# Extra products of constants on TensorE inside its waits, in a two-model transformer kernel on one Trainium2 core

## The chip, the cores and the metric

The kernel runs on one core of a Trainium2 chip. Its time is the device time of one launch in microseconds (us). Three runs of the kernel before gave 2714.12 us as their median, from 2710.6 to 2715.03 us.

## What is computed

A sequence of 256 tokens of width 1024 passes through two models, all in float32. The first has two layers; each is a SwiGLU feed-forward network (1024 to 2816 and back), a mixer, a cross attention to 256 memory tokens, and a second feed-forward network, with an RMS norm ahead of each part. The mixer of layer 0 has windowed attention with sinks beside stick-breaking attention; that of layer 1 is a dilated attention with 16 heads. The second model has two layers whose norms are scaled and shifted by vectors made from a conditioning input. Its mixer is a hybrid of three attentions, and after it comes a dense feed-forward network in layer 0 and a mixture of 8 experts, two per token, in layer 1. Cut to what matters:

```python
for layer in range(2):                       # first model
    x = x + 0.5 * swiglu_ffn(rms_norm(x), ...)
    x = x + mixer[layer](rms_norm(x), ...)
    x = x + memory_cross_attention(rms_norm(x), mem, ...)
    x = x + 0.5 * swiglu_ffn(rms_norm(x), ...)
for layer in range(2):                       # second model
    h = rms_norm(x) * (1 + sc1) + sh1
    x = x + gt1 * hybrid_mixer(h, ...)
    h = rms_norm(x) * (1 + sc2) + sh2
    x = x + gt2 * (swiglu(h, ...) if layer == 0 else moe_swiglu(h, ...))
return rms_norm(x)
```

## The kernel before, in words

A plan (`make_plan`) lists the stages in order, and every engine has its own program that walks through that list; semaphores tie the programs together. Tokens are held in two row tiles (b = 0, 1) of 128 each, and the width in 8 blocks (k) of 128. Weights stream through a ring of seven 1 MB slots (ten in the experts) that SyncE fills; a slot is refilled when TensorE has used what was in it. PSUM has eight banks of 128x512 float32, and each stage has a fixed use of them. One matmul of float32 stands in the trace as two instructions of the same shape; counts such as x16 are of those.

TensorE's program, the only one that the change touches, is one strict order of instructions:

- **norm** (L1112). For each row tile it waits for x (`x_at`), then turns 8 blocks of x (L1108, 16 instructions) into banks 0 to 3. In an "early" norm it then waits for VectorE's diagonal matrix of the row scales (L2504), multiplies it by ones (L1119) into bank 7, and the next stage starts. VectorE copies that row (L2507) and writes xT block by block (L2513, and L2518 where there is a shift); the next stage's first products (L1231 of a feed-forward network, L1815 of the hybrid mixer) follow block by block on the count `xT_k`. The norms ahead of the feed-forward networks and of the hybrid mixers are early, seven in all. The others ("late") apply the row scale afterwards; the one ahead of the router is "raw".
- **feed-forward** (L1217): the first pair of tiles by plain products (L1231 gate, L1234 up), then a seven-product form (L1274), then the product with the second weight (L1325).
- **attn** (L1584), the attentions with sinks (4 bodies of two heads) and dilated (8 bodies). Staged copies of queries and keys, made by GpSimd, are turned (L1577) into banks 4 and 5; scores (L1603) go to banks 0 and 1; weights are turned (L1617) into banks 2 and 3; outputs (L1629) go to bank 6. Pieces of the memory's keys and values for the later cross attention (`kv_piece`, L1553, bank 7) stand between these steps: one piece (sinks) or two (dilated) before body 0, and the others beside the bodies.
- **stick** (L1650), stick-breaking attention, with the later-sums (L1682) into banks 2 and 3.
- **hybrid** (L1798): pieces of the input projection (L1815, banks 5 and 7), ten pairs of heads, and pieces of the output projection (L1836). At pair 5, `turn_diff` (L1907) waits for `diff_done`, VectorE's normalised output of the difference heads (L2676), turns it (L1912) into bank 5, and then come scores (L1893) of pair 6.
- **route and experts**: 16 products with 8 columns for the router (L2022), a wait for `chosen_ready` (VectorE's choice of experts), five products with 8 columns (L2002 to L2006), the gathering products of expert 0 (L1369), whose results ScalarE moves to SBUF (L2279), and then the experts' products (L1418, L1461), whose weights come at the rate of the DMA.

`cst` is a table of constants in SBUF, loaded at the kernel's start, and `ident` its first 128 columns. A wait of TensorE's program holds back all that stands behind it, as here in `outputs` of attn:

```python
                    for b in range(NB):
                        pe.wait_ge(sm[f"p_ready{b}"], w + 1)     # L1613: exponentials are there
                        pe.wait_ge(sm[f"pt_evac{b}"], w)         # L1614: bank 2 + b is free
```

Of the kernel before, what the change touches and what calls it, by code (L numbers as in the profile page):

```python
# [423 lines left out]
def build(nc, A, out, stop=None):  # L424
    plan, released, landed, places, before = make_plan(stop)
    ctx = ExitStack()
    with ctx:
# [668 lines left out]
        def _(pe):  # L1096
# [3 lines left out]
            def transposes_of(src, done, ready=None):  # L1100

                rows = src.rearrange("p b (q k) -> p b k q", k=KT)
                for b in range(NB):
                    if ready is not None:
                        ready(b)
                    for half in range(2):
                        for j in range(4):
                            ins = nc.tensor.transpose(banks[2 * b + half][:, j * P:(j + 1) * P],  # L1108
                                                      rows[:, b, half * 4 + j, :], ident)
                        ins.then_inc(done, 1)  # L1110

            def norm(st):  # L1112
                n0 = st["n0"]
                last = [max(i for i, (pb, _) in enumerate(pieces(st["order"])) if pb == b) for b in range(NB)]
                transposes_of(x[:, :, :], sm["norm_psum"], lambda b: x_at(pe, st, last[b]))
                if st["how"] == "early":
                    pe.wait_ge(sm["diag_ready"], st["early"] + 1)
                    for b in range(NB):
                        ins = mm(banks[7][:, b * P:(b + 1) * P], C("ones"), diag[:, b, :], start=True, stop=True)  # L1119
                    ins.then_inc(sm["rsb_psum"], 1)  # L1120

# [234 lines left out]
            def experts(st):  # L1356
# [42 lines left out]
                def gate_up(e, i, between):  # L1399
                    n, groups = 3 * e + i, GROUPS_OF[e]  # L1400
                    w = CHUNKS[i][1]
                    for k in range(KT):
# [3 lines left out]
                        if k == 0:  # L1406
                            pe.wait_ge(sm["gath_evac"], 2 * (e + 1))
# [176 lines left out]
            def attn(st):  # L1584
# [7 lines left out]
                def scores(i):  # L1592
# [3 lines left out]
                    staged_out(u)  # L1596
                    for b in range(NB):
                        pe.wait_ge(sm[f"s_read{b}"], w)

# [8 lines left out]
                def outputs(i):  # L1608
                    u, w = i + st["n0"]["pairs"], i + st["n0"]["soft"]
                    beside(i, 2, 6)  # L1610
                    for b in range(NB):
                        nt = b + 1
                        pe.wait_ge(sm[f"p_ready{b}"], w + 1)  # L1613
                        pe.wait_ge(sm[f"pt_evac{b}"], w)  # L1614
# [20 lines left out]
                for n in side["first"]:  # L1635
                    kv_piece(st, n, 0, KT)
                scores(0)
# [12 lines left out]
            def stick(st):  # L1650
# [24 lines left out]
                def later(i):  # L1675

                    w = i + n0["stick"]
                    for h in range(2):
                        pe.wait_ge(sm[f"sp_done{h}"], w + 1)
                        pe.wait_ge(sm[f"arg_done{h}"], w)  # L1680
# [117 lines left out]
            def hybrid(st):  # L1798
# [108 lines left out]
                def turn_diff():  # L1907
                    pe.wait_ge(sm["diff_done"], l + 1)
                    pe.wait_ge(sm["w2_evac0"], nb * (l + 1))
# [66 lines left out]
            for i_st, st in enumerate(plan):  # L1976
# [3 lines left out]
                if kind == "norm":  # L1980
                    norm(st)
# [17 lines left out]
                elif kind == "experts":  # L1999

                    pe.wait_ge(sm["chosen_ready"], 1)
# [1537 lines left out]
```

## Time and profile before

| what | us |
|---|---|
| median of three runs (lowest, highest) | 2714.12 (2710.6, 2715.03) |
| time of the profiled execution | 2716.32 |
| its span, first to last instruction | 2714.4 |
| TensorE busy | 2573.7 (95%) |
| VectorE busy | 1291.6 (48%) |
| ScalarE busy | 438.0 (16%) |
| GpSimd busy | 200.9 (7%) |
| mean granted TensorE clock | 0.983 of full speed |
| HBM traffic over the span | 227 GB/s |

1.9 us of the profiled execution's time lie outside its span. The page also has the busy share and TensorE's granted clock by fortieths of the span, and the chain of work that ended last. Other views used below: the timeline (start, duration, engine, line, operation, out<-in, shapes, count; in brackets the engine's idle time before it and what ended that), the waits of an engine, and windows, which give each engine's busy time, the granted clock, the DMA share and GB/s in a stretch.

### The profile page before, as it was taken

What the parts mean: (1) busy time and instruction counts of PE and PEld (TensorE: products, weight loads), DVE (VectorE), ACT (ScalarE), POOL (GpSimd) and SP (SyncE); (2) the same over time, 40 slices, a digit from 0 to 9 for tenths busy, and PEclk for the clock granted to TensorE, in tenths of its full rate; (3) what the DMA queues carried; (4) which work ended last, traced back from release to release, by engine and by line L of the source; (5) the groups of instructions that cost most, each with busy time, mean ns of one, the idle gap of its engine ahead of it and who ended that gap; (6) DMA issues with size and microseconds to landing.
All of it is one profiled execution on the core that took longest, in us unless ns stands there. A gap on an engine that the chain in (4) does not pass through costs nothing.

```text
span 2714.4 us, 44439 instructions
## 1 busy us (share of the span) xinstructions
PE 2573.7 (95%) x18246; PEld 1684.7 (62%) x18246; DVE 1291.6 (48%) x2756; ACT 438.0 (16%) x1199; POOL 200.9 (7%) x330
## 2 busy tenths in 40 slices
PE   8999899999999998999999989999989999989996
PEld 8964457797599444577964659945655335624452
DVE  5887342478877854325887536664531000000102
ACT  1201252010012013221101321102311001101010
POOL 3010100000000102000011110001100000000000
PEclk9999999999999999999999999999989999999999
DMA  8684323367556733234675324543359999999997
GB/s 286 212 312 161 109 94 124 114 218 251 208 194 229 245 139 124 79 108 149 218 258 149 123 101 164 181 161 114 116 186 382 413 412 413 416 413 411 411 414 314
DMA packets 306524, 619.19 MB, mean 228 GB/s; under 512 B 15948, under 2 KB 172784, under 8 KB 306192
## 3 DMA queue, kind: packets, MB, share of 16 engines
q1 hardware_dynamic: 287088, 550.80, 54.9%
q0 software_dynamic: 19232, 65.52, 7.4%
q8 instruction: 147, 2.41, 0.3%
q14 instruction: 57, 0.47, 0.1%
HBM read 607.47 MB, written 8.79 MB: 227 GB/s over the span
## 4 chain that ended last, share of the span: by engine, by line
PE 69%; issue 10%; DVE 9%; DMA 6%; SPq 3%; ACT 1%; POOL 1%; DVEq 0%; POOLq 0%; ACTq 0%
PE psum L1274 22%; PE psum L1418 10%; PE psum L1815 6%; PE psum L1461 5%; PE psum L1325 4%; PE psum L1553 3%; DMA xn<-in_w_ada 2%; PE psum L1190 2%; PE psum L1142 2%; PE psum L1726 2%; PE psum L1836 2%; DMA ring<-in_w_exp_up 2%; PE psum L1231 2%; DVE proj L2874 1%; DMA ring<-in_w_exp_down 1%
## 5 line engine op out<-in xcount | busy, mean ns | idle before, releaser
L1418 PE MATMUL psum<-ring,xT 128*32 128x512 f32 (+3 forms) x3372 | 293.3, 494 | 15.6 <-DMA ring<-in_w_exp_up 13.9
L3370 DVE SCALAR_TENSOR_TENSOR proj<-proj,psum 128x256 f32<-128x256 f32 (+1 forms) x63 | 24.8, 394 | 558.1 <-ACT proj L2294 558.1
L1418 PEld LDWEIGHTS psum<-ring,xT 128*32 128x32 f32 x3372 | 129.3, 110 | 166.5 <-issue 114.2
L1274 PE MATMUL psum<-xT,ring 128*128 128x128 f32 x1600 | 195.0, 275 | 0.0
L1274 PEld LDWEIGHTS psum<-xT,ring 128*128 128x128 f32 x1600 | 187.7, 192 | 4.1 <-issue 3.8
L1815 PE MATMUL psum<-ring,xT 128*128 128x384 f32 (+1 forms) x448 | 157.8, 502 | 2.9 <-DVE xT L2518 2.9
L2874 DVE SCALAR_TENSOR_TENSOR proj<-xn,cols,proj 128x512 f32<-128x512 f32 x168 | 126.0, 750 | 17.6 <-DMA xn<-in_w_ada 13.5
L1553 PE MATMUL psum<-ring,memT 128*128 128x512 f32 x256 | 121.4, 614 | 7.3 <-issue 7.3
L1815 PEld LDWEIGHTS psum<-ring,xT 128*128 128x128 f32 x448 | 82.3, 192 | 61.9 <-issue 13.6
L938 POOL DMA_DIRECT2D xn<-in_w_ada x96 | 69.4, 724 | 686.5 <-DVE proj L2874 679.9
L1461 PE MATMUL psum<-ring,proj 128*32 128x256 f32 x1872 | 104.6, 379 | 0.0
L1325 PE MATMUL psum<-ring,proj 128*128 128x512 f32 x220 | 102.6, 592 | 0.0
L1274 PE MATMUL psum<-qT,ring 128*128 128x128 f32 x800 | 98.0, 276 | 1.4 <-DVE picked L3068 1.4
L1274 PE MATMUL psum<-diff_o,ring 128*128 128x128 f32 x800 | 97.5, 275 | 0.0
L1274 PEld LDWEIGHTS psum<-qT,ring 128*128 128x128 f32 x800 | 93.3, 192 | 5.6 <-DVE picked L3068 5.6
L1461 PEld LDWEIGHTS psum<-ring,proj 128*32 128x32 f32 x1872 | 73.8, 110 | 31.5 <-issue 6.1
L1274 PEld LDWEIGHTS psum<-diff_o,ring 128*128 128x128 f32 x800 | 93.3, 192 | 0.0
L2187 ACT ACTIVATE silu<-pT 128x256 f32<-128x256 f32 x100 | 41.8, 418 | 292.8 <-DVE pT L2996 185.1
L1553 PEld LDWEIGHTS psum<-ring,memT 128*128 128x128 f32 x256 | 47.2, 196 | 58.7 <-issue 58.4
L2294 ACT ACTIVATE proj<-psum 128x256 f32<-128x256 f32 (+1 forms) x63 | 23.0, 366 | 345.3 <-PE psum L1418 345.3
L1325 PEld LDWEIGHTS psum<-ring,proj 128*128 128x128 f32 x220 | 41.4, 190 | 50.2 <-issue 50.2
L1836 PE MATMUL psum<-ring,memT 128*128 128x512 f32 x128 | 63.4, 630 | 0.9 <-ACT memT L2092 0.9
(534 smaller groups left out, 4287.6 us busy)
## 6 DMA issues: line engine op xcount, KB each, us to landing
ring<-in_ffn_w_gu SPq DMA_DIRECT2D x88, 1024.0 KB, 7.3
ring<-in_w_exp_down SPq DMA_DIRECT2D x62, 1024.0 KB, 16.8
xn<-in_w_ada POOLq DMA_DIRECT2D x96, 512.0 KB, 4.8
ring<-in_ffn_w_down SPq DMA_DIRECT2D x44, 1024.0 KB, 7.7
ring<-in_w_exp_gate SPq DMA_DIRECT2D x82, 512.0 KB, 11.5
ring<-in_w_exp_up SPq DMA_DIRECT2D x82, 512.0 KB, 15.5
ring<-in_w_exp_gate SPq DMA_DIRECT2D x52, 384.0 KB, 9.8
ring<-in_w_exp_up SPq DMA_DIRECT2D x52, 384.0 KB, 12.4
```

The lines of the kernel that those rows point to most:

```text
L938: nc.gpsimd.dma_start(ada_slot[a % 2], wv[:, 2 * q:2 * q + 2, half * 3072 + c * 512:half * 3072 + (c + 1) * 512])\
L1142: ins = mm(banks[4 + 2 * s + b][:, 0:w], lhsT(k, b), wt[:, k - i * ks, :], start=(k == 0), stop=(k == KT - 1))
L1190: ins = mm(banks[bank][:, :], tokens[:, k, :], w[:, k, :], start=(new and k == 0), stop=(k == 3), skip_group_check=True)
L1231: mm(banks[4 + f][:, 0:S], gate[:, k, f * P:(f + 1) * P], xT[:, k, :], start=(k == 0), stop=(k == KT - 1))
L1274: ins = mm(banks[bank][:, t * P:(t + 1) * P], weights(t)[:, k, :], tokens[:, k, :], start=(new and t == 0 and k == 0), stop=(k == 3), skip ...
L1325: ins = mm(banks[bank][:, :], tokens, weights, start=(d == 0), stop=last, skip_group_check=True)
L1418: ins = mm(o[:, :, o0:o1], xg[e % 2][:, k, 32 * g:32 * g + 32], w_[:, :, c0:c1], start=(k == 0 and n_ == 0), stop=(k == KT - 1), skip_grou ...
L1461: ins = mm(bank[32 * g:32 * g + 32, at:at + 256], tokens[:, 32 * tg:32 * tg + 32], wt[:, f, d0:d0 + 256], start=first and at == 0, stop=la ...
L1553: ins = mm(banks[7][:, :], memT[:, k, b * P:(b + 1) * P], slot(u).rearrange("p (k n) -> p k n", k=4)[:, k % 4, :], start=(k == 0), stop=(k ...
L1815: ins = mm(banks[(5, 7)[b]][:, 0:w], xT[:, k, b * P:(b + 1) * P], slot(u)[:, 0:4 * w].rearrange("p (k n) -> p k n", k=4)[:, k % 4, :], sta ...
L1836: ins = mm(banks[(7, 5, 0, 4)[n]][:, :], yTh[:, k, b * P:(b + 1) * P], slot(u).rearrange("p (k n) -> p k n", k=4)[:, k % 4, :], start=(k = ...
L2874: ins = V.scalar_tensor_tensor(ada_sum, w, cols[:, 16 + k:17 + k], ada_sum, ALU.mult, ALU.add)
```

## The change

A helper `keep_busy(bank, n)` issues n products of `ident` (128x128) with the first 512 columns of `cst` into a PSUM bank whose content nobody needs at that time; nothing reads the result. It is called in these places: in every early norm but the first, once after the turns and once after the product with the diagonal (12 products); at the head of a norm that follows a hybrid mixer (2); between the two row tiles of the norm that follows the dense feed-forward network (2); before body 0 of the two attentions (3 each) and between the two pieces of the dilated one (1); before the scores of body 1 (both attentions) and 7 (3); before the first turn of body 7 (1); before the first later-sum of stick (1); in `turn_diff` (2 in each layer); before the wait for the choice of experts (3), and before the first expert's first product (1). That is 36 products. Where the bank's release was waited for after another event, the two waits change places, so that the release comes first. Nothing else is touched: no other engine's program and no DMA.

```diff
@@ 1097 @@
-def transposes_of(src, done, ready=None):
+def keep_busy(bank, n):
+    for _ in range(n):
+        mm(banks[bank][:, :], ident, cst[:, 0:512], start=True, stop=True, skip_group_check=True)
+def transposes_of(src, done, ready=None, between=None):
@@ 1108 @@
             ins.then_inc(done, 1)
-def norm(st):
+        if b == 0 and between is not None:
+            between()
+def norm(st, after):
     n0 = st["n0"]
+    if after["kind"] == "hybrid":
+        keep_busy(6, 1)
     last = [max(i for i, (pb, _) in enumerate(pieces(st["order"])) if pb == b) for b in range(NB)]
-    transposes_of(x[:, :, :], sm["norm_psum"], lambda b: x_at(pe, st, last[b]))
+    transposes_of(x[:, :, :], sm["norm_psum"], lambda b: x_at(pe, st, last[b]),
+                  (lambda: keep_busy(4, 2)) if after.get("out") == "gated" else None)
     if st["how"] == "early":
+        if n0["norm"]:
+            keep_busy(6, 1)
         pe.wait_ge(sm["diag_ready"], st["early"] + 1)
...
         ins.then_inc(sm["rsb_psum"], 1)
+        if n0["norm"]:
+            keep_busy(6, 1)
@@ 1404 @@
             if k == 0:
+                if n == 0:
+                    keep_busy(0, 1)
                 pe.wait_ge(sm["gath_evac"], 2 * (e + 1))
@@ 1593 @@
         beside(i - 1, 0, 2)
-        staged_out(u)
         for b in range(NB):
             pe.wait_ge(sm[f"s_read{b}"], w)
+        if "side" in st and i in (1, 7):
+            keep_busy(0, 1)
+        staged_out(u)
@@ 1610 @@
             nt = b + 1
+            pe.wait_ge(sm[f"pt_evac{b}"], w)
+            if i == 7 and b == 0:
+                keep_busy(2, 1)
             pe.wait_ge(sm[f"p_ready{b}"], w + 1)
-            pe.wait_ge(sm[f"pt_evac{b}"], w)
             for h in range(heads):
@@ 1633 @@
     for n in side["first"]:
+        if n:
+            keep_busy(4, 1)
         kv_piece(st, n, 0, KT)
+    if side["first"]:
+        keep_busy(4, 3)
     scores(0)
@@ 1676 @@
         for h in range(2):
+            pe.wait_ge(sm[f"arg_done{h}"], w)
+            if i == 0 and h == 0:
+                keep_busy(2, 1)
             pe.wait_ge(sm[f"sp_done{h}"], w + 1)
-            pe.wait_ge(sm[f"arg_done{h}"], w)
             sp_t = stick_sp[i % 2][h]
@@ 1905 @@
     def turn_diff():
+        pe.wait_ge(sm["w2_evac0"], nb * (l + 1))
+        keep_busy(5, 2)
         pe.wait_ge(sm["diff_done"], l + 1)
-        pe.wait_ge(sm["w2_evac0"], nb * (l + 1))
         for t in range(2):
@@ 1978 @@
     if kind == "norm":
-        norm(st)
+        norm(st, plan[i_st - 1] if i_st else {"kind": None})
     elif kind == "xattn":
@@ 1998 @@
+        keep_busy(0, 3)
         pe.wait_ge(sm["chosen_ready"], 1)
```

## Rows read from the trace of the kernel before

**Rows 1.** The page: granted clock by fortieths; shares of the chain that ended last.
```profile
PEclk9999999999999999999999999999989999999999
...
PE 69%; issue 10%; DVE 9%; DMA 6%; SPq 3%; ACT 1%; POOL 1%; DVEq 0%; POOLq 0%; ACTq 0%
```

**Rows 2.** Windows over the 16 stretches at granted clock 0.50: first, last, and their sum.
```profile
core 0: us, PE busy (x) PEld busy (x) DVE busy (x) ACT busy (x) POOL busy (x), PEclk, DMA share, GB/s
302.60:306.00 3.40, 3.40 (x11) 1.90 (x8) 2.62 (x7) 0.73 (x4) 0.95 (x2) 0.51 0.00 0
...
2709.00:2714.40 5.40, 0.00 (x0) 0.00 (x0) 2.35 (x2) 0.00 (x0) 0.00 (x0) 0.50 0.48 197
sum 90.90, PE 71.73 PEld 45.60 DVE 53.16 ACT 6.11 POOL 10.41; mean PE 4.48 PEld 2.85 DVE 3.32 ACT 0.38 POOL 0.65
```

**Rows 3.** Timeline of an early norm, ahead of the first layer's second feed-forward network.
```profile
502.87 2.11 PE L1108 MATMUL psum<-cst,x 128*128 128x128 f32 x16
...
506.30 0.71 PE L1119 MATMUL psum<-diag,cst 128*128 128x128 f32 x4 [1.32 <-DVE diag L2504]
...
507.51 3.23 DVE L2513 SCALAR_TENSOR_TENSOR xT<-psum,gains,rs_row 128x256 f32<-128x256 f32 x8
...
508.14 6.72 PE L1231 MATMUL psum<-xT,ring 128*128 128x256 f32 x16 [1.13 <-DVE xT L2513]
...
514.69 3.62 PE L1234 MATMUL psum<-xT,ring 128*128 128x256 f32 x16
```

**Rows 4.** Timelines of the next early norms' first products; the last is of the dense network.
```profile
729.75 5.16 PE L1231 MATMUL psum<-xT,ring 128*128 128x256 f32 x16 [1.13 <-DVE xT L2513]
...
1244.18 5.38 PE L1231 MATMUL psum<-xT,ring 128*128 128x256 f32 x16 [1.13 <-DVE xT L2513]
...
1623.93 6.26 PE L1231 MATMUL psum<-xT,ring 128*128 128x256 f32 x16 [1.79 <-DVE xT L2518]
...
1629.08 0.35 DVE L2518 TENSOR_SCALAR xT<-xT,mod_shift 128x256 f32<-128x256 f32 x1
```

**Rows 5.** Timeline of the norm ahead of the second hybrid mixer.
```profile
1839.27 1.22 PE L1119 MATMUL psum<-diag,cst 128*128 128x128 f32 x4 [0.29 <-DVE diag L2504]
...
1846.99 0.35 DVE L2518 TENSOR_SCALAR xT<-xT,mod_shift 128x256 f32<-128x256 f32 x1
...
1850.03 0.63 DVE L2603 COPY proj<-psum 128x452 f32<-128x452 f32 x1 [0.80 <-PE psum L1815]
```

**Rows 6.** Waits of TensorE (us in total, times, longest): before body 0 with sinks.
```profile
PE psum L1577 <- POOL k_st L1080: 3.1, 1, 3.1
```

**Rows 7.** Timelines of the two attentions: with sinks, then dilated (three rows).
```profile
309.71 5.26 PE L1553 MATMUL psum<-ring,memT 128*128 128x512 f32 x8
...
1046.11 1.65 PE L1603 MATMUL psum<-kTt,qT 64*128 64x128 f32 x8 [0.56 <-ACT qT L2363]
...
1052.92 0.93 PE L1603 MATMUL psum<-kTt,qT 64*128 64x128 f32 x8 [1.66 <-ACT qT L2363]
...
1126.25 2.86 PE L1629 MATMUL psum<-proj,pT 128*128 128x64 f32 x12
```

**Rows 8.** Timeline of the first hybrid mixer, from the turn of the difference heads.
```profile
1566.68 1.12 PE L1912 MATMUL psum<-cst,y 128*128 128x128 f32 x4 [2.87 <-DVE y L2676]
...
1567.73 1.66 PE L1893 MATMUL psum<-qT 64*128 64x128 f32 x8
...
1569.32 3.50 PE L1836 MATMUL psum<-ring,memT 128*128 128x512 f32 x4
...
1577.70 1.98 PE L1836 MATMUL psum<-ring,memT 128*128 128x512 f32 x4
```

**Rows 9.** Timeline of the routing and the first expert's first products.
```profile
1998.86 3.72 PE L2022 MATMUL psum<-lamv,xT 128*128 128x8 f32 x32
...
2005.46 0.59 PE L2002 MATMUL psum<-chosen,cst 128*128 128x8 f32 x2 [2.88 <-DVE chosen L3510]
...
2008.72 5.69 PE L1369 MATMUL psum<-p_sb,y 128*128 128x96 f32 x32 [0.96 <-DVE p_sb L3308]
...
2015.99 9.63 PE L1418 MATMUL psum<-ring,xT 128*32 128x512 f32 x72 [1.58 <-ACT xT L2279]
```

**Rows 10.** Timeline, SyncE's first refill in the experts; windows, a stretch of the experts.
```profile
2020.52 0.33 SPq L817 DMA_DIRECT2D ring<-in_w_exp_gate  x1
...
2100.00:2200.00 100.00, 92.56 (x986) 34.13 (x985) 8.20 (x21) 9.29 (x27) 1.64 (x3) 1.00 1.03 415
```

## The prediction

> **What bounds the kernel now.** I read the page first. The chain that ended last is 69% TensorE, and TensorE's granted clock is printed as full in all but one fortieth [rows 1]; so TensorE's own pace sets the time, and what is to be gained by a faster clock is small. The windows over the stretches at half clock tell how small [rows 2]. There are 16 of them, 90.9 us together, each at 0.50, which is 1.2 GHz where the rest runs at 2.4. TensorE is busy in 71.7 us of them. The last, 5.4 us, holds no matmul. So 72 us of work at half clock would take about 36 us at full clock: 36 us, 1.3% of the time, is the ceiling of any change to the clock.
>
> The timelines then tell what TensorE did before the clock fell. Ahead of the second feed-forward network it turned x, waited 1.32 us for VectorE's diagonal, ran 0.71 us of small products, waited 1.13 us, and at 507.4 the clock was at half when the first large products began [rows 3]. It is the same at 729.3 and 1244.7 [rows 4]. The hybrid mixers fall after the 2.87 us wait for the difference heads [rows 8], the routing after 3.7 us of products with 8 columns [rows 9], the attentions after the 3.1 us wait for GpSimd [rows 6]. Fourteen stretches thus lie at or just behind a thin place, and twelve of those places get extra products. Two lie in the experts (2385 and 2651), where TensorE waits for weights; the change leaves these.
>
> **What one extra product costs.** Each is one 128x512 float32 product, two instructions. Four such instructions took 1.98 us at full clock, with the 0.2 us that the last one's end stands out, and 3.50 at half [rows 8]: one product is 0.86 us at full clock and 1.7 us at half. The 36 are 31 us at full clock, and 61 us at half. What hides them is the wait in which each stands; if it did not, all 31 us would be on the path.
>
> - Norms: one product in the 1.32 us wait and one in the 1.13 us wait [rows 3]: hidden at full clock, with 0.3 to 0.4 us left. At half clock they would be late by 0.4 and 0.6 us.
> - Attentions: three (2.6 us) in the 3.1 us wait before body 0 [rows 6], one in the 1.66 us wait before the scores [rows 7].
> - Difference heads: two (1.7 us) in the 2.87 us wait [rows 8]; w2_evac0, now waited for first, was long there. Queued behind `diff_done` are the turn, the scores and the output pieces; they are free when they were.
> - Routing: three (2.6 us) in the 2.88 us wait for `chosen` [rows 9]. Here the thin stretch lies ahead of them, so the clock is already at half when they start. At 1.7 us each they last 5.1 us, 2.2 us past the wait, less if the clock comes back on the way. I take 1.7 us late. One more lies in the 1.58 us wait before the first expert's products.
> - The remaining six stand in similar waits (for x between row tiles, for the memory's keys, body 7, the first later-sum). I cost them at nothing; bound from above, half a product each, 2.6 us. A reordered wait costs nothing: both were waited for anyway.
>
> The chip's order of matmuls matters here. In the timelines no matmul starts ahead of an earlier one, and so I let every late product push what follows. The Trainium skill (TensorE: Matmul & The Clock Gate, section on what overlaps in packed matmuls) says the same, strict order with only weight loads pulled ahead; it would make every product that outlasts its wait a loss.
>
> **What the kept clock gives back, place by place.** In each the question is who paces the work once TensorE is fast.
>
> 1. Second feed-forward network: the first 16 instructions run from 508.14 to 514.69, 6.55 us. VectorE writes the eight blocks in 3.23 us, to 510.74; one more block's product, 0.45 us, gives 511.2. Gain 3.5 us [rows 3]. By the same working, with 0.17 us of each duration overlapping the next group, the stretches at 729.75 and 1244.18 last 4.99 and 5.21 us against 3.05: gains 1.9 and 2.2 [rows 4]. Behind them TensorE had no other idle time for 30 us, and so nothing swallows this. Together 7.6.
> 2. Dense network: VectorE makes two passes per block and ends its last at 1629.43; the group ends at 1630.02 [rows 4]. It is VectorE that paces it: gain 0.1 us.
> 3. Second hybrid mixer: the product with the diagonal takes 1.22 us instead of 0.71, 0.5 us on the path. The first piece ends about 1849.9 (VectorE's copy waited for it until 1850.03), while the last block was ready at 1847.34. Half a microsecond earlier and with a last product of 0.76 us (452 of 512 columns of 0.86 us) it would end at 1847.6 [rows 5]. Gain 2.2 us.
> 4. Attentions: the eight instructions at 309.71 take 5.26 us, at full clock twice 1.8: 1.6 us, and the turns behind them had ScalarE waiting [rows 7, 8]. In the dilated one the first scores take 1.65 us instead of 0.93, with the turns ahead 1.0 us [rows 7]. At its end the outputs take 2.86 us where half would do, and then turns and the first products of the next stage lie at half clock too, some 3.3 us in all [rows 7]. That stretch is thin in itself, so I expect one extra product to keep only part: 2.3. Together 4.9.
> 5. Difference heads: 1.12 us against some 0.6, 1.66 against 0.93, 3.50 against 1.98 [rows 7, 8]: 2.7 us, and VectorE waited for these scores. The second layer does the same after its wait, at 1945, and its stretch at half clock is as long: 2.7. Together 5.4.
> 6. Routing: the five small products and the gathering products now start 1.7 us late but run at full clock. The five take about 1.2 us instead of 2.3; the 32 gathering instructions take 5.69 us, at full clock about 3.9 at the 0.12 us spacing of the turns [rows 3, 9]. Net 1.1 + 1.8 - 1.7 = 1.2. The first expert's first block releases its slot at 2020.52, 4.5 us after its start at 2015.99; at full clock the 24 instructions of a block take 2.6 us (48 in the 5.1 us that are left of the 9.63) [rows 9, 10]. Gain 1.9. Together 3.1.
>
> The experts that follow are at the rate of the DMA: 415 GB/s and all engines busy in 2100 to 2200 [rows 10]. That doesn't take the gain away, since this DMA stream starts with the release at 2020.52 and so shifts with it. It does mean that the two falls within it cost nothing.
>
> The sum: 7.6 + 0.1 + 2.2 + 4.9 + 5.4 + 3.1 = 23.3 us, against the profiled execution's 2716.3 (span 2714.4 and 1.9 around it): 2693.0. The runs' median is 2714.1, 2.2 lower, so this execution probably had a little more half clock than the middle one. I take 2694.
>
> **Rivals.**
>
> - **A: the clock holds at some places only.** A gap with one product of 0.86 us in it is still thin, and the fall then comes a little later, on the same large products. The 1.13 us wait with 0.86 us of it filled speaks against; the turns of the attentions' ends speak for. If it holds at half the places, half of 23.3: 2704. Chance 0.14.
> - **B: others pace the work.** As in the dense network [rows 4], VectorE, ScalarE or GpSimd decide how soon the next product may start, and TensorE waits longer where it was slow before. Against: in groups 1 and 5 the other engines were the ones that waited. If only these norms' and routing's shares (7.6 + 3.1) stay: 2705. Chance 0.12.
> - **C: slower, by late products.** Place: the two waits of each norm, 1.32 and 1.13 us. If the extra products don't hold the clock, each takes 1.7 us there and is late by 0.4 and 0.6 us. Over six norms that is 6 us, the difference heads' two outlast their wait by 0.5 each, and routing is 2.2 late: 9 us, with the gain gone, 2723. It decides from the point at which the clock is at half when the norm's first extra product starts; in rows 3 it was still full. Chance 0.05.
> - **D: the change doesn't do what it says**, because the clock doesn't answer to it, or its record is wrong. The durations in rows 7 and 8 (3.50 and 1.98 for the same four instructions) show that the record is right. The Trainium skill (TensorE: Matmul & The Clock Gate, section "Seeing it yourself") warns that such clock events were seen to be unreliable; by that rule the 90.9 us of half clock would not be there and the change would give 2714 or a little more. The trace disagrees. Chance 0.05, at 2714 to 2717.
>
> **How the numbers follow.** The forecast (most stretches gone, sum as above) has the remaining 0.64, with its own range of 2688 to 2700: the lower end if the last attention's stretch is held in full and the median execution gains as the profiled one, the upper if the six uncosted products cost 2.6 us and routing gives nothing. The range of 8 in 10 takes in A and B: 2687 to 2707. A measurement of this kernel can tell about 0.2%, 5.4 us, from no change, so "same" is 2708.7 to 2719.5. D, and the far ends of A and B, make 0.11; C makes 0.05; faster is 0.84.
>
> **What would show it.** The mean granted clock should rise from 0.983 to about 0.993, with half-clock stretches left at 2385, 2651 and the end, at the routing (around the three products), and perhaps near 1125. L1231 after the norms should take about 3.2 us for 16 instructions in place of 5 to 6.7, L1912 0.6 us, the four L1836 behind it 2.0 us, and the first release in the experts should stand 4.5 us or less behind a start that itself is some 20 us earlier. The waits before L1119 should shrink to about 0.3 us and no norm's diagonal product should start later after VectorE's diagonal than now. Wrong would be: half clock at the same places in spite of the products, or L1231 just as long at full clock.

## The result, and the profile after

The changed kernel takes 2698.4 us (median of six runs, 2694.51 to 2701.36) against 2714.14 us of the kernel before, timed beside it: ratio 0.9946, 95% interval 0.9933 to 0.9958, 14.7 us faster. The forecast was 2694 us, with a range of 2687 to 2707. The profiled execution took 2700.31 us, its span is 2698.5 us, and the mean granted clock 0.996. The page answers to [rows 1]:

```profile
span 2698.5 us, 44578 instructions
...
PEclk9999999999999999999999999999999999999999
```

Windows over the five stretches at half clock that are left, which answer to [rows 2]:

```profile
1046.50:1049.90 3.40, 3.16 (x10) 1.77 (x11) 1.89 (x7) 0.18 (x1) 0.00 (x0) 0.53 0.00 0
1985.10:1992.00 6.90, 6.90 (x17) 3.82 (x17) 2.49 (x16) 1.98 (x3) 0.00 (x0) 0.52 1.03 418
1995.40:1998.80 3.40, 3.40 (x19) 3.40 (x19) 2.88 (x17) 1.40 (x4) 0.00 (x0) 0.53 0.00 0
2640.50:2643.90 3.40, 3.40 (x24) 0.85 (x20) 1.09 (x3) 0.77 (x2) 0.00 (x0) 0.54 1.02 414
2691.70:2698.50 6.80, 0.00 (x0) 0.00 (x0) 2.64 (x3) 0.20 (x2) 0.72 (x1) 0.52 0.39 157
sum 23.90, PE 16.86 PEld 9.83 DVE 11.00 ACT 4.53 POOL 0.72; mean PE 3.37 PEld 1.97 DVE 2.20 ACT 0.91 POOL 0.14
```

90.9 us have become 23.9. One of the five lies in the dilated attention, two in the routing, one in the experts and one at the end. The timeline of the norm of [rows 3] now reads (L1103 are the extra products, L1131 is what was L1119, L1245 was L1231, L1248 was L1234):

```profile
502.88 2.11 PE L1113 MATMUL psum<-cst,x 128*128 128x128 f32 x16
...
504.82 1.02 PE L1103 MATMUL psum<-cst 128*128 128x512 f32 x2
...
506.30 0.71 PE L1131 MATMUL psum<-diag,cst 128*128 128x128 f32 x4 [0.46 <-DVE diag L2532]
506.85 1.02 PE L1103 MATMUL psum<-cst 128*128 128x512 f32 x2
...
508.14 3.69 PE L1245 MATMUL psum<-xT,ring 128*128 128x256 f32 x16 [0.27 <-DVE xT L2541]
...
511.67 3.62 PE L1248 MATMUL psum<-xT,ring 128*128 128x256 f32 x16
```

Both extra products fit: the waits shrink from 1.32 to 0.46 us and from 1.13 to 0.27, and the instructions behind them start at the very times of before. The first group lasts 3.53 us (508.14 to 511.67), not 6.55. The difference heads, against [rows 8]:

```profile
1555.00 1.88 PE L1103 MATMUL psum<-cst 128*128 128x512 f32 x4
1558.03 0.66 PE L1939 MATMUL psum<-cst,y 128*128 128x128 f32 x4 [1.15 <-DVE y L2704]
1558.61 0.93 PE L1919 MATMUL psum<-qT 64*128 64x128 f32 x8
1559.47 1.98 PE L1862 MATMUL psum<-ring,memT 128*128 128x512 f32 x4
```

The wait is 1.15 us instead of 2.87, and the three groups behind it take 0.66, 0.93 and 1.98 us instead of 1.12, 1.66 and 3.50. The routing, against [rows 9], shows the opposite:

```profile
1982.52 4.38 PE L2050 MATMUL psum<-lamv,xT 128*128 128x8 f32 x32
1986.76 5.47 PE L1103 MATMUL psum<-cst 128*128 128x512 f32 x6
...
1989.56 0.17 DVE L3538 TENSOR_TENSOR chosen<-s_sb 128x16 f32<-128x16 f32 x1
...
1992.02 0.38 PE L2030 MATMUL psum<-chosen,cst 128*128 128x8 f32 x2
...
1994.26 5.41 PE L1383 MATMUL psum<-p_sb,y 128*128 128x96 f32 x32 [0.96 <-DVE p_sb L3336]
...
2001.16 7.93 PE L1434 MATMUL psum<-ring,xT 128*32 128x512 f32 x72 [0.60 <-ACT xT L2307]
```

The clock fell while the router's products with 8 columns ran, so that the three extra products, meant for the wait, took 5.47 us and ended 2.3 us after `chosen` was there (1989.56 + 0.17 to 1992.02). It fell again in the gathering (L1383), which took 5.41 us. From the router's first product to the first expert's it is now 18.64 us (1982.52 to 2001.16) where it was 17.13.

**Where the time went, place by place.** Each entry compares, in the two profiled executions, the time from the same instruction ahead of a place to the same one behind it (for the first: 6.55 - 3.53 = 3.02).

```
place                                         predicted   measured, us gained
norms ahead of L1231: 508, 730, 1244          3.5 1.9 2.2  3.0  1.5  1.7
norm of the dense network                     0.1          0.0
norm of the second hybrid mixer               2.2          2.1
attention with sinks                          1.6          2.0
dilated attention, start                      1.0         -0.6
dilated attention, end and next stage         2.3          3.1
difference heads, first and second layer      2.7  2.7     2.7  2.95
routing to the first release of a ring slot   3.1          0.2
sum                                           23.3         18.6
all other stages                              0           -2.7
```

The last line is no place of the change. Most of it stands in the feed-forward networks, where TensorE waits for VectorE's sums for the conditioning vectors (L1298 before, L1312 after), whose inputs come by GpSimd's DMA: these waits are 4.9 us in all before and 6.4 after. They differ from one execution to the next, also with the same code (e8 6.9 us, e12 10.3), and the clock may fall behind them; the trace of e12 has an instance (below). That the difference of 2.7 us has nothing to do with the change is likely by this, but not shown.

This table compares one execution with one other. The traces of the experiments below, which have the same code at most of these places, show what of it is chance; a second table, behind them, puts them side by side.

### The profile page after: what moved, and what is told of

The parts are those of the page before. It is cut to its first block, busy times and chain, and to the rows that moved or that the text cites. A ratio compares the mean times of both kernels' runs of the same rounds, so it can differ in the third digit from the quotient of the medians.

```text
span 2698.5 us, 44578 instructions
## 1 busy us (share of the span) xinstructions
PE 2580.1 (96%) x18318; PEld 1677.5 (62%) x18318; DVE 1291.7 (48%) x2756; ACT 438.6 (16%) x1199; POOL 201.0 (7%) x330
## 3 DMA queue, kind: packets, MB, share of 16 engines
HBM read 607.47 MB, written 8.79 MB: 228 GB/s over the span
## 4 chain that ended last, share of the span: by engine, by line
PE 68%; issue 10%; DVE 9%; DMA 6%; SPq 4%; ACT 1%; POOL 1%; DVEq 0%; POOLq 0%; ACTq 0%
PE psum L1288 22%; PE psum L1434 10%; PE psum L1841 6%; PE psum L1477 5%; PE psum L1339 4%; PE psum L1569 3%; DMA xn<-in_w_ada 2%; PE psum L1204 2%; PE psum L1752 2%; PE psum L1156 2%; PE psum L1862 2%; DMA ring<-in_w_exp_up 2%; SPq L817 2%; DVE proj L2902 1%; PE psum L1245 1%
## 5 line engine op out<-in xcount | busy, mean ns | idle before, releaser
L1434 PE MATMUL psum<-ring,xT 128*32 128x512 f32 (+3 forms) x3372 | 291.5, 492 | 18.4 <-DMA ring<-in_w_exp_up 17.4
L1569 PE MATMUL psum<-ring,memT 128*128 128x512 f32 x256 | 118.9, 603 | 6.4 <-issue 6.4
L2976 DVE TENSOR_TENSOR ring<-ring 128x512 f32<-128x512 f32 x100 | 64.2, 683 | 0.0
```

What stands on the lines that cost most here:

```text
L1434: ins = mm(o[:, :, o0:o1], xg[e % 2][:, k, 32 * g:32 * g + 32], w_[:, :, c0:c1], start=(k == 0 and n_ == 0), stop=(k == KT - 1), skip_grou ...
L1569: ins = mm(banks[7][:, :], memT[:, k, b * P:(b + 1) * P], slot(u).rearrange("p (k n) -> p k n", k=4)[:, k % 4, :], start=(k == 0), stop=(k ...
L2976: ins = V.tensor_tensor(A21, A11, A21, ALU.subtract)
```

## Experiments

Each was timed beside the kernel before. The clock given with a time is the median of the mean clocks of that kernel's runs. The kernel before ran 52 times in these sessions: median clock 0.985; the 14 executions at 0.983 or less took 2716.3 us on average, the 17 at 0.986 or more 2711.4.

**e1, only the norms' products.** The four calls of `norm` stay, all others are removed.

```diff
-                keep_busy(4, 3)
-                    keep_busy(5, 2)
-                    keep_busy(0, 3)
...
```

> Only the 16 products in the norms stay; those of the attentions, the later-sum, the difference heads, the routing and the first expert are gone. Theory (each place gives back what its own half-clock stretch cost, and places are independent): the norms' terms of the prediction are 7.6 + 0.1 + 2.2 = 9.9 us, in the changed kernel's trace they measured about 9; so 8 to 10 us faster than before, 6 us slower than the whole change, half clock back at the attentions, the difference heads and the routing. Rival (other engines pace the work behind the norms, and what was gained comes from the other places): 2 to 4 us faster than before.

Measured: 2708.38 us, ratio 0.9983 (0.9974 to 0.9992), 4.6 us faster (2.2 to 7.1); clock 0.989. Place by place its trace shows the norms' 3.0, 1.5, 1.7 and 2.1 us again, 8.3 in all, measured against the profiled execution of before. The timed gain is about half of that, below the 8 to 10 us of the theory and just above the 2 to 4 of the rival. What the rival says, that other engines pace the work, is not what the trace shows. The profiled execution of before was dearer at the norms than others are: the traces of e2 and e7, whose norms have no extra products either, lost 6.5 us (0, 1.7, 1.7 and 3.1) and 3.8 us (1.7, 0, 0 and 2.1) at the same four places.

**e2, all but the norms' products.** The four calls of `norm` are removed.

> The whole change without its 16 products in the norms. Theory: the gain left is the changed kernel's 15.7 us less the norms' 9, so 5 to 8 us faster than before; L1245's kind (16 instructions after an early norm) lasts 5 to 6.7 us again where the clock falls. If places were not independent (a clock kept at one place shifts the fall to the next), the sum of this gain and of the norms alone would be far from 15.7 us.

Measured: 2702.45 us, ratio 0.9965 (0.9954 to 0.9976), 9.5 us faster (6.5 to 12.5), more than the 5 to 8 expected; clock 0.990. With e1 that makes 14.1 us, against 14.7 of the whole: the places are independent within what can be measured, which is some 5 us. In its trace the clock held behind one norm without any extra product:

```profile
505.97 3.69 PE L1239 MATMUL psum<-xT,ring 128*128 128x256 f32 x16 [1.13 <-DVE xT L2535]
```

The stretch from that norm's first turn to the end of this group is 8.80 us, as with the two products in the changed kernel. So two products that fit into their waits cost nothing, and their gain is nothing in an execution in which the clock would have held there.

**e3, the same products with 8 columns.**

```diff
-mm(banks[bank][:, :], ident, cst[:, 0:512], ...)
+mm(banks[bank][:, 0:8], ident, cst[:, 0:8], ...)
```

> All 36 products stay where they are, with the same banks and the same order of waits, but each has 8 columns in place of 512. Theory (what helps is the streaming of columns, which keeps the clock): no gain, within 2 us of the kernel before, mean clock near 0.983, the same places at half clock. Rival (the reordered waits, or instructions issued ahead of a wait, make TensorE start sooner): the gain of 15 us stays, with the clock low.

Measured: 2710.22 us, ratio 0.9989 (0.998 to 0.9998), 3 us faster (0.5 to 5.4), barely outside the noise and a little more than the 2 us expected at most; clock 0.985, as before. Its norm at 508 us:

```profile
507.08 0.71 PE L1131 MATMUL psum<-diag,cst 128*128 128x128 f32 x4 [1.21 <-DVE diag L2532]
507.63 0.29 PE L1103 MATMUL psum<-cst 128*128 128x8 f32 x2
508.92 5.18 PE L1245 MATMUL psum<-xT,ring 128*128 128x256 f32 x16 [1.00 <-DVE xT L2541]
```

The products are there, the order of waits is the new one, and the group behind is slow as ever (5.18 us). So most of the gain doesn't come from issuing something ahead of a wait or from the moved waits, but from the length of the products. Where the 3 us come from, if they are no chance, isn't shown. The stretches that its trace has at half clock are those of before and some more, 102 us in all.

**e4, without the products at the routing and the first expert.**

```diff
-                                keep_busy(0, 1)
...
-                    keep_busy(0, 3)
```

> The whole change without the three products ahead of the choice of experts and the one ahead of the first expert. In the changed kernel's trace the first ran at half clock, lasted 5.2 us and held the next products back 2.3 us, and the clock fell once more in the gathering. Theory A (the three cost what they give): within 1.5 us of the whole change. Theory B (as predicted, routing gains 3.1 us): 3 us slower than the whole change. Theory C (they are a loss): 2 us faster than the whole change.

Measured: 2697.08 us, ratio 0.9944 (0.993 to 0.9957), clock 0.995: the whole change to within its noise. That is nearest to theory A, but the intervals (11.7 to 19.0 us faster than before, and 11.4 to 18.2 for the whole change) leave room for the 3 us of B and the 2 of C. In this trace the routing has half clock from 1988.6 to 1998.8, and the choice is not held back:

```profile
1990.25 0.59 PE L2027 MATMUL psum<-chosen,cst 128*128 128x8 f32 x2 [2.89 <-DVE chosen L3535]
...
1993.51 6.32 PE L1383 MATMUL psum<-p_sb,y 128*128 128x96 f32 x32 [0.96 <-DVE p_sb L3333]
```

**e5, one product amid the router's and one ahead of the gathering.**

```diff
+                        if b:
+                            keep_busy(7, 1)
                         for k in range(KT):
...
+                    keep_busy(0, 1)
                     experts(st)
```

> The whole change, with two more products: one between the two row tiles of the router's products (8 columns each), which are the thin stretch after which the clock falls, and one behind the five small products, ahead of the gathering. Theory (the router's own products let the clock fall, so the three that come after them run at half clock): the clock now stays full through the routing; the first addition costs 0.9 us of the path, the three products take 2.6 us and are no longer late (they were by 2.3), the 32 gathering instructions fall from 5.4 to about 4 us. In the trace, from the end of the router's products to the first expert's first product 3 to 4 us less than in the changed kernel, net 2 to 3 us faster: ratio to before near 0.9935. Rival (the gathering is paced by something else than the clock): the three are on time, but the gathering still takes 5.4 us; net 1 us.

Measured: 2699.21 us, ratio 0.995 (0.9932 to 0.9968). In its profiled execution the routing was 2.5 us shorter than in the changed kernel's, but the three products still ran mostly at half clock:

```profile
1981.18 1.10 PE L1103 MATMUL psum<-cst 128*128 128x512 f32 x2
1982.12 2.16 PE L2053 MATMUL psum<-lamv,xT 128*128 128x8 f32 x16
1984.13 4.20 PE L1103 MATMUL psum<-cst 128*128 128x512 f32 x6
```

In that execution one product in the thin stretch didn't hold the clock: it fell at 1983.5, before the router's last products were done. The 2 to 3 us expected don't show in the timing, whose interval (8.7 to 18.4 us faster than before) doesn't exclude them.

**e6, two products in each wait of the norms.** `keep_busy(6, 1)` becomes `keep_busy(6, 2)` at both places of an early norm.

> The whole change with two products instead of one in each of the two waits of the six early norms. Theory (matmuls keep strict order, a product that outlasts its wait is late by the difference): two last 1.7 us at full clock, 0.4 us past the 1.32 us wait and 0.6 us past the 1.13 us one; so about 1 us lost per norm, 6 us slower than the whole change. Rival (part of such a product is hidden by the pipeline, or the later one eats slack of VectorE's chain): 2 us or less slower.

Measured: 2699.79 us, ratio 0.9947 (0.9927 to 0.9967), clock 0.995: the same as the whole change, and not 6 us slower. Place by place the norms at 504 and 723 us are 0.48 us longer each, the one at 1233 is 0.71 longer and the dense network's not at all, where 1.0 each was expected:

```profile
502.31 2.09 PE L1113 MATMUL psum<-cst,x 128*128 128x128 f32 x16
...
505.96 0.61 PE L1131 MATMUL psum<-diag,cst 128*128 128x128 f32 x4
...
506.41 1.88 PE L1103 MATMUL psum<-cst 128*128 128x512 f32 x4
...
508.13 3.62 PE L1245 MATMUL psum<-xT,ring 128*128 128x256 f32 x16
511.58 3.62 PE L1248 MATMUL psum<-xT,ring 128*128 128x256 f32 x16
```

Late products do push what follows. Counted from the first turn (502.31 here, 502.88 in the changed kernel), the product with the diagonal starts 0.23 us later (3.65 for 3.42), the first group 0.56 later (5.82 for 5.26), and the group ends 0.48 later (9.27 for 8.79), since it finds blocks ready and takes 3.45 us for 3.53. The expected 0.4 and 0.6 us were both too much: the idle time in brackets begins at the end of the instruction before it, and a further product starts some 0.16 us ahead of that end (508.13 is 1.72 us behind 506.41, whose group lasts 1.88).

**e7, only the difference heads' products**, four of 36.

> Only the two products in each turn of the difference heads stay, 4 of 36. Theory: 5.4 us by the prediction and 5.7 by the changed kernel's trace (2.7 and 3.0 in its two places), where the clock falls in the kernel before; since it falls there in most but perhaps not in all executions, 4 to 5.7 us faster than before. Rival (places depend on each other): under 2 us.

Measured: 2707.14 us, ratio 0.998 (0.9967 to 0.9993), 5.4 us faster (1.9 to 9.0); the trace shows 2.7 and 2.95 us at the two places. As predicted, and the best return of any place: these four of 36 products give about a third of the gain.

**e8, two products before the scores of body 1.**

```diff
-                        keep_busy(0, 1)
+                        keep_busy(0, 2 if i == 1 else 1)
```

> The whole change with two products instead of one before the scores of body 1 of both attentions, where the wait left is 1.5 and 1.0 us after the first. Theory (at 1046 us of the changed kernel the clock fell because one product in that gap is too little): no half clock at body 1 of either attention, the scores take 0.93 us again and the following eight instructions 3.7 instead of 4.6; 0 to 2 us faster than the whole change at that place, nothing at the others. Rival: the fall there only depends on where it happens to stand in an execution, and the second product does nothing or is late by 0.2 us.

Measured: 2697.05 us, ratio 0.9938 (0.9915 to 0.996), clock 0.996. In the dilated attention the changed kernel had, and e8 has (the second fence is e8's):

```profile
1044.62 1.10 PE L1103 MATMUL psum<-cst 128*128 128x512 f32 x2 [0.89 <-DVE s_sb L2783]
1046.74 1.65 PE L1621 MATMUL psum<-kTt,qT 64*128 64x128 f32 x8 [1.02 <-ACT qT L2391]
1048.32 4.58 PE L1569 MATMUL psum<-ring,memT 128*128 128x512 f32 x8
```

```profile
1045.47 1.95 PE L1103 MATMUL psum<-cst 128*128 128x512 f32 x4 [0.89 <-DVE s_sb L2783]
1047.59 0.93 PE L1621 MATMUL psum<-kTt,qT 64*128 64x128 f32 x8 [0.16 <-ACT qT L2391]
1048.44 3.70 PE L1569 MATMUL psum<-ring,memT 128*128 128x512 f32 x8
```

The second product is on time with 0.16 us to spare, and the place is 1.6 us shorter than in the changed kernel's execution. But that isn't the second product's doing, as far as the traces go: six others with a single product there (e2, e4, e5, e6, e9, e10) kept the clock as well and take the same 22.2 us for the stretch that begins at 1034.12 and ends at 1057.31 in the kernel before. Here is e4's, with one:

```profile
1049.06 0.93 PE L1619 MATMUL psum<-kTt,qT 64*128 64x128 f32 x8 [1.02 <-ACT qT L2388]
1049.92 3.70 PE L1567 MATMUL psum<-ring,memT 128*128 128x512 f32 x8
```

So the rival stands: whether the clock falls there depends on the execution, and nothing shows that the second product does anything. The same execution of e8 shows the routing wholly at full clock, without any edit there:

```profile
1984.02 3.72 PE L2050 MATMUL psum<-lamv,xT 128*128 128x8 f32 x32
1987.59 2.82 PE L1103 MATMUL psum<-cst 128*128 128x512 f32 x6
1990.62 0.39 PE L2030 MATMUL psum<-chosen,cst 128*128 128x8 f32 x2 [0.20 <-DVE chosen L3538]
...
1992.86 3.78 PE L1383 MATMUL psum<-p_sb,y 128*128 128x96 f32 x32 [0.96 <-DVE p_sb L3336]
...
1998.13 7.93 PE L1434 MATMUL psum<-ring,xT 128*32 128x512 f32 x72 [0.60 <-ACT xT L2307]
```

14.11 us from the router's first product to the first expert's, 4.5 less than in the changed kernel with identical code there. Whether a thin stretch makes the clock fall differs from one execution to the next; in the routing e8's is the only one of all traces without a fall. That e8 is faster than the whole change isn't shown by the timing; the intervals overlap.

**e9 and e10, one of the norms' two products.** e9 removes the one behind the diagonal's product, e10 the one ahead of it.

> The whole change without the second product of each early norm (the one behind the product with the diagonal); the first, in the 1.32 us wait, stays. [...] Rival (the last product before the large ones is what counts): as without any, 5 us slower, clock 0.990.

> The whole change without the first product of each early norm; the second, in the 1.13 us wait, stays. [...] Rival (the last product before the large ones is what counts): no slower than the whole change.

Measured: e9 2700.56 us, ratio 0.995 (0.9934 to 0.9967), clock 0.994, with half clock behind three of the six norms in its trace (1456, 1613 and 1831 us), which costs 1.6 us at each of the two hybrid mixers and nothing at the dense network; e10 2697.94 us, ratio 0.9938 (0.9922 to 0.9955), clock 0.995, with none behind a norm. The product that stands next to the large ones does as well alone as both; the other way round it looks worse in the trace, but the times don't separate the two. e9's clock of 0.994 isn't the 0.990 that its rival expects, so the last product ahead of the large ones isn't the only one that counts.

**e11, 256 columns in place of 512.**

> All 36 products with 256 columns in place of 512. With 8 columns nothing was kept (mean clock 0.985 as before), with 512 it is 0.995. Theory (streamed columns count, and 512 is not far above what is needed in the norms): in between, clock about 0.991, 8 to 11 us faster than before. Rival (a product of any real width will do): as the whole change, 0.995 and 15 us.

Measured: 2700.34 us, ratio 0.9948 (0.993 to 0.9966), but clock 0.992. With 8, 256 and 512 columns the clock is 0.985, 0.992 and 0.9955. The clock is as the theory says, in between. The time is the rival's, 14.1 us faster than before, but its interval (9.2 to 19.0) takes in most of the theory's 8 to 11 us as well; the timing doesn't decide between them. Its trace held the clock behind the norms of the feed-forward networks and lost it behind those of the two hybrid mixers.

**e12, e8 with a product ahead of each half of the router's products and one ahead of the gathering.**

> The whole change, with two products before the scores of body 1, one product ahead of each of the router's two row tiles, and one ahead of the gathering. Theory (the routing's stretch was only diluted by a single product in its middle, where the clock fell in the profiled execution; two products in it keep the clock at a price of 1.7 us on the path): no half clock between the norm and the first expert; the three products on time, 4.5 us gained behind them and 1.7 paid; clock 0.996 to 0.997, 2 to 3 us faster than the whole change. Rival: the two products cost as much as they give, and it stands where the whole change with body 1 doubled stood (2697).

Measured: 2697.81 us, ratio 0.9936 (0.992 to 0.9951), clock 0.995: where the rival has it, though the 2 to 3 us of the theory aren't excluded. In its trace the clock fell just as the three products began (4.52 us long), after two others had stood among the router's, so that part of the theory fails in that execution. The same trace has the loss outside the change that was named above:

```profile
704.65 3.11 DVE L2904 SCALAR_TENSOR_TENSOR proj<-xn,cols,proj 128x512 f32<-128x512 f32 x4 [2.60 <-DMA xn<-in_w_ada]
...
707.91 2.05 PE L1312 MATMUL psum<-proj,cst 128*128 128x512 f32 x2 [2.59 <-DVE proj L2904]
709.75 1.71 PE L1339 MATMUL psum<-ring,p_sb 128*128 128x512 f32 x2
```

VectorE waits 2.60 us for its input, TensorE 2.59 us for VectorE's sum (in the changed kernel's execution at most 0.8 us in that network), and the clock falls at once. That one place takes 3.4 us more than in the changed kernel's execution.

**The same places in all traces.** Each figure is again the time from one instruction to another, the same in every kernel, in us. "With" are the traces whose code at that place is the changed kernel's.

```
place                    without extra products         with them
norm at 504              11.8 (before) 8.8 (e2)         8.8 in all
                         10.5 (e7)
norm at 726              10.3, 10.6, 8.9 (the same)     8.9 in all
norm at 1241             10.2, 10.3, 8.6                8.6 in all
norm, second hybrid      19.2, 20.3, 19.2               17.1 in all
attention with sinks     24.2 (before) 26.4 (e1)        22.2 in five, 23.8 in two (e5, e9)
                         23.6 (e7)
dilated, start           23.2, 23.4, 23.1               22.2 in six, 23.8 in one (after)
dilated, end             24.1, 22.9, 23.6               20.9 in four, 21.8 in five
difference heads, both   19.1 (before) 18.0 (e1)        13.5 in all
routing to the 25th      21.4, 21.4, 21.3 (e7)          21.2 (after) 21.2 (e6)
instruction of L1418     20.3 (e4)                      19.6 (e2, e9, e10) 16.7 (e8)
```

## Why the prediction was right, and where its sizes were off

The direction, the mechanism and the range held. Extra products in the waits keep the clock, and their length is what does it (e3), they are hidden by the waits (0.46 and 0.27 us are left in a norm, and e2's norm took as long without them), and the places add up (e1 and e2). The size was too large: a sum of 23.3 us, and 20 between the median and the forecast of 2694, against 15.7 between the medians. The result lies near the upper end of the forecast's own 2688 to 2700, which the prediction gave to a routing without gain; in the profiled execution that is what happened. By its own steps:

1. **Cost of a product**, 0.86 and 1.7 us: right. Six instructions took 2.82 us at full clock and 5.47 mostly at half.
2. **Norms**, 9.9: 8.3. The gain of the first three was worked out with VectorE as the pace (3.05 us a group). At full clock the group takes 3.53: a block's two instructions, 0.43 us together, take a little longer than VectorE's 0.40, so TensorE still paces, and each gain is about 0.5 us too large. The dense network, where VectorE does pace, gave nothing, as said. The larger error lies in the execution read: in the mean of the three traces without norm products (before, e2, e7) the norms' places lose 6.2 us, and 4.6 timed (e1).
3. **Attentions**, 4.9: 4.5. In the changed kernel's execution the clock fell again at body 1 of the dilated one (-0.6 for 1.0), and its end was held in full (3.1 for 2.3). Over the traces of the second table both terms are about as predicted: 1.0 us at the start in six of seven, and at the end 2.1 in the mean.
4. **Difference heads**, 5.4: 5.65, and 5.4 timed alone (e7), the place where trace and timing agree best.
5. **Routing**, 3.1: 0.2. This is the term that was furthest off. The prediction had the three products late by 1.7 us (2.3 measured) and then the gathering at full clock. But behind the five products with 8 columns the clock was at half once more, so the 1.8 us of the gathering came to 0.3, and not only here: it was so in five of the six traces with these products (after, e2, e6, e9, e10; not e8). Their six differ by 4.5 us, and in the mean the place is 1.5 us shorter than in the four without: half of the term. e4's timing is too coarse to add to this. At full clock throughout, the place is worth 4.7 us (e8: 3.0 up to the first expert, 1.7 behind).
6. **One execution read as the typical one.** The prediction noted that the profiled execution was 2.2 us above the median and took 2694 in place of 2693, but it sized each term by the falls of that execution. Its clock was 0.983; the middle is 0.985, which over the span is 2 x 0.002 x 2714 = 11 us less at half clock. At the norms this shows: 8.3 us in the profiled pair, 6.5 and 3.8 in e2's and e7's traces, 4.6 timed (e1).

Two counts of the prediction are off without moving its sum. Of the 16 stretches 15 hold matmuls and 13 of these lie outside the experts, where it says fourteen. And the products that it costs at nothing are eight, not six: the two at the head of a norm that follows a hybrid mixer are missing. In the changed kernel's trace the one at 1978.32 ends ahead of a wait of 0.73 us for x, so that it cost nothing.

The ceiling of 36 us assumed that TensorE paces all of its 72 busy microseconds at half clock. From 0.985 to 0.9955 the change took away 2 x 0.0105 x 2714 = 57 us of half clock for 14.7 us, a quarter of a microsecond for each, where pure pacing would give a half.

Rival A was right about the routing, where the clock fell in all traces but e8's, and in single executions of the attentions; B about the dense network alone; C's mechanism was seen at the routing only, and e6 shows that even doubled products in the norms cost 0.5 to 0.7 us a norm, not 1; D is excluded by e3, where the same places without the length have the clock and nearly the time of before. No version is shown faster than the whole change: e8, e10 and e12 stand at 0.9936 to 0.9938 with intervals that take in 0.9946. e10 does with six products fewer what the whole change does.

What stays open: whether any filling would keep the router's stretch at full clock (two products did not in the execution profiled); how often each place falls in the kernel before, for which the two to four traces without products at a place are few; and why the places' 18.6 us in the profiled pair, and about as much in the means of the second table, are more than the 14.7 timed (11.4 to 18.2). Several traces have falls at other places (near 700 and 930 us, in feed-forward networks, and near 1092 us, in the dilated attention) that the profiled executions of the two kernels lack; they may take a part of it.

## What to carry to other kernels

Look at the granted clock in windows before believing that TensorE is fully fast: here 91 of 2714 us were at half, nearly all just behind short waits of 1 to 3 us among small products, and a product of constants that fits into such a wait costs nothing and gives back what the large products behind it lose. Put it next to the large products (e10's trace has no fall behind a norm, e9's three, though their times don't differ clearly), size it by the wait at half clock if small products lie ahead of it, and expect a quarter of a microsecond per microsecond of half clock removed, since other engines pace part of that work. Whether a given place falls changes from execution to execution, so take the sizes from the mean clock of many runs and from several traces, before one of a pair is taken for the effect of the change: one body of the dilated attention looked like a failure of the change in one trace and like its mending in the next, and six other traces say that it was neither.

## What the runs showed of the hardware

- Products with 8 columns did not hold the clock, though TensorE was busy all the time. In the changed kernel's execution TensorE had no idle time from 1981.40 us on, first with 8 turns and then with the router's 34 instructions of 8 columns, and the clock fell at 1985.4, amid them. It fell amid them in five of the twelve traces whose router stands alone (after, e1, e6, e7, e11), at their end or within 1.4 us behind them in five, was at half already in one (e3) and held in one (e8). And 36 extra products with 8 columns left the mean clock at 0.985 (e3).
- Identical code met different clocks: the routing took 18.64 us in the changed kernel's execution and 14.11 us in e8's. The Trainium skill (TensorE: Matmul & The Clock Gate, section "What's actually happening") says that the point at which the clock changes varies from run to run; the trace agrees.
- A product that overhangs its wait costs less than the overhang that the brackets suggest: two more products in a norm, about 1 us of overhang by the brackets, made it 0.48 us longer (e6), since a product starts about 0.16 us ahead of the end that is shown for the one before it.
